# Cache copies by whole rows in packets of 8192 bytes, some of them moved to ScalarE's queue, and later turns in a hybrid decoder step

## Chip, core and metric

The kernel runs on one core of a Trainium2 chip. The metric is the device time of one execution in microseconds (us); lower is better.

## What is computed

One layer of a hybrid decoder, for a prompt group (1 x 512 tokens) and a sample group (8 sequences x 4 tokens, with a past of 2048 rows). In the reference, shortened:

```python
def hybrid_mixer(h, w_in, ..., hist):
    proj = h @ w_in                                   # q, k, v, z, xbc, dt: 1024 -> 5648
    att = [dilated attention(q, k_all, v_all, w, d) for w, d in ((128,1),(512,4),(2048,16))]
    att_out = mix_dilations(att)
    y, h_last = ssd_scan(conv(xbc), dt, A, Bm, Cm, D, h0, chunk)
    out = concat[att_out, gated_rmsnorm(y, z, g)] @ w_out
    keep = max(0, k_all.shape[1] - MAX_WINDOW)
    new_state = (k_all[:, keep:], v_all[:, keep:], ...)   # sample: old cache moved up by 4 rows, 4 new rows
# h <- LN1(ALPHA*h + mixer(h));  h <- LN2(ALPHA*h + PEER(h))
# PEER: queries, top 16 of 128 x 128 product keys, 8 heads, gelu(tok . u[e]) * gate, sum of v[e]
```

For the sample group each new cache (keys and values) is (8, 2048, 1024) in float32: rows 4 to 2047 of the old cache become rows 0 to 2043 of the new one, and four new rows follow. These 2044 rows of 4096 bytes per sequence, for keys and for values, are copied from DRAM to DRAM; nothing in the kernel computes with the copied rows.

## The kernel before, in words

Each engine runs one program of stages, in this order: projections (`sp_project`, `act_project`, `pool_project`, `dve_project`, `pe_project`), attention (`*_attend`), the SSD scan (`*_ssd_run`, `sp_ssd`), the output product with LN1 (`*_out`), the PEER queries with top-k (`*_query`, `dve_topk`), the dense up product beside one-hot gates (`*_up`, `dve_onehots`), and the values product with LN2 (`*_values`, `*_final`). Engines wait for each other on semaphores only.

Weights are float32 split in a high and a low part. SyncE loads a block of 128 x 1024 (512 KB) of w_in into one of four slots, L300; ScalarE rounds it (`hi`, L326), GpSimd subtracts (`lo`, L363), and TensorE multiplies it in three products (`product`, L188 to L190). There are 44 blocks, eleven turns of four slots. ScalarE's cast of block j waits until TensorE has released the slot, so at most four blocks are ahead. The tokens (xraw) are loaded in two halves of four chunks each, L293 and L295, the dt weight between them; ScalarE rounds chunk by chunk (L318, L321), VectorE subtracts (L377, L380).

The cache copies. 2044 rows x 1024 floats per sequence are taken as one run and cut into 16 units (`CHUNK`, L269), a unit into 16 pieces of 32704 bytes. `copy_cache` (L272 to L277) copies one unit of all 8 sequences, with the pieces as outermost dimension, then the sequences: 128 packets of 32704 bytes. `copy_half` (L279 to L283) copies half a unit of the values, 128 packets of 16352 bytes. All add to the semaphore `copied`, and only SyncE's last wait of `sp_values` (L2193) waits for it, for all 48. Where they are issued:

- ScalarE's queue, in `act_project`: after each turn of four weight casts, `copies(x)` (L328) issues a unit of keys and half a unit of values, ten times.
- SyncE's queue: four halves at the end of `sp_attend` (L643); in `sp_ssd` (L981), after the norm gain and the first two states, six units of keys and a half (L987 to L989); in `sp_out`, two halves after each of the first two pairs of w_out loads (L1451, L1452); in `sp_query` a half ahead of each of the twelve later peer_wq loads and one before them (L1623, L1626).

An issue occupies the queue of the engine that makes it; the instructions after it on that engine stand behind it. SyncE does nothing but waits and issues. ScalarE also has the casts, the exponentials of the attention and the copies out of PSUM.

Attention is a loop of 67 rounds (`ROUNDS`): scores of unit n, transposes of unit n-2, values of unit n-3, with the steps of the eight sample sequences between (`sample_steps`). In round `EVERY + 4` of a sequence `dec_turn_out` (L736) turns its output; it waits for VectorE's `d_rows`, and stands ahead of the round's own turn and values.

The SSD scan works on four chunks of 128 tokens and the sample rows. Orders are written out by hand in `pe_ssd`, `act_ssd` and `dve_ssd` (L936 to L950). TensorE's `turn_out` (L1031) transposes the normed rows of chunk i-1 at the end of the loop body of chunk i (L1148). VectorE's `dve_ssd_run` begins with a wait for the norm gain (L1245), which it first uses in `normed` (L1314). In `act_query` (L1700) ScalarE copies each of the 16 queries out of PSUM and rounds a later weight block.

Of the kernel before, what the change touches and what calls it, by code (L numbers as in the profile page):

```python
# [16 lines left out]
D = 1024  # L17
# [131 lines left out]
def layer(nc, t):  # L149

    ctx = ExitStack()
    with ctx:
# [92 lines left out]
        x_in = [sem(f"x_in{s}") for s in range(2)]  # L245
# [23 lines left out]
        CHUNK = (WIN - NT) * D // 16  # L269
        PIECE = CHUNK // 16  # L270

        def copy_cache(eng, side, x):  # L272

            src, dst = (("cache_k", "o_ks"), ("cache_vall", "o_vsall"))[side]
            cutout = lambda ap, lo: ap.rearrange("b s d -> b (s d)")[:, bass.ds(x * CHUNK + lo, CHUNK)]\
                .rearrange("b (s n) -> s b n", n=PIECE)
            eng.dma_start(cutout(t[dst], 0), cutout(t[src], NT * D)).then_inc(copied, 16)  # L277

        def copy_half(eng, y):  # L279

            cutout = lambda ap, lo: ap.rearrange("b s d -> b (s d)")[:, bass.ds(y * (CHUNK // 2) + lo, CHUNK // 2)]\
                .rearrange("b (s n) -> s b n", n=PIECE // 2)
            eng.dma_start(cutout(t["o_vsall"], 0), cutout(t["cache_vall"], NT * D)).then_inc(copied, 16)  # L283

# [5 lines left out]
        def sp_project(sp):  # L292
            sp.dma_start(xraw[:, 0:4], t["xT"][:, 0:4]).then_inc(x_in[0], 16)  # L293
            sp.dma_start(dtw_raw, t["w_dt"]).then_inc(dtw_in, 16)
            sp.dma_start(xraw[:, 4:8], t["xT"][:, 4:8]).then_inc(x_in[1], 16)  # L295
# [19 lines left out]
        def act_project(act):  # L315
            for c in range(DC):
                act.wait_ge(x_in[c // 4], 16)
                act.copy(xs[0][:, c], xraw[:, c]).then_inc(x_hi, 1)  # L318
                if c == 3:
                    act.wait_ge(dtw_in, 16)  # L320
                    act.copy(dtw[0], dtw_raw).then_inc(x_hi, 1)  # L321
# [6 lines left out]
            def copies(x):  # L328
                copy_cache(act, 0, x)
                copy_half(act, x)  # L330
# [17 lines left out]
            with act.Fori(0, 2) as x:  # L348
                for s in range(4):
                    hi(x + 8, s, (rows_ready, x * 10 + (5 if s < 2 else 10)))  # L350
                copies(x + 8)
            for s in range(4):
                hi(10, s, (rows_ready, 20 + (5 if s < 2 else 10)))
# [3 lines left out]
        def pool_project(pool):  # L357
# [9 lines left out]
            pool.wait_ge(x_in[0], 16)  # L367
            pool.wait_ge(x_in[1], 16)
# [5 lines left out]
        def dve_split_x(dve):  # L374
            for c in range(DC):
# [2118 lines left out]
```

## Time and profile before

| what | value |
|---|---|
| median of 3 runs | 2127.38 us (2119.74 to 2133.82) |
| profiled execution, in all | 2123.87 us |
| its span | 2122.0 us |
| PE busy | 2027.4 us (96%) |
| PE weight load busy | 1687.3 us (80%) |
| DVE, ACT, POOL busy | 1488.1, 743.7, 784.4 us |
| bytes moved by DMA | 683.04 MB, mean 322 GB/s |
| HBM read, written | 618.78, 196.32 MB |

PE is TensorE's matmul, DVE VectorE, ACT ScalarE, POOL GpSimd, SP SyncE; SPq and ACTq are the instructions of an engine's queue that issue DMAs, and are not counted as busy. L12 is line 12 of the kernel. A DMA share of 1.00 is all sixteen DMA engines busy. MB and GB are powers of ten; KB of an issue is 1024 bytes. The span runs from the first to the last instruction in the profile.

### The profile page before, as it was taken

The numbers are of one execution on the slowest core, as the hardware profiler recorded it, in microseconds if no ns is written. First come the engines' busy times: TensorE is split into PE (matmuls) and PEld (weight loads), VectorE is DVE, ScalarE is ACT, GpSimd is POOL, SyncE is SP. The second block draws the span as 40 slices with busy tenths as digits, with TensorE's granted clock in tenths as the row PEclk, the third lists the DMA queues.
The fourth block names the chain that finished last, engine by engine and source line by source line (L and its number), as shares of the span: only waits on it lengthen the run. The fifth ranks groups of instructions, "written<-read, shape, count | busy, mean of one in ns | idle before, by whom it ended". The sixth has DMA issues, their size and how long they took to land.

```text
span 2122.0 us, 33482 instructions
## 1 busy us (share of the span) xinstructions
PE 2027.4 (96%) x12142; PEld 1687.3 (80%) x12142; DVE 1488.1 (70%) x3108; ACT 743.7 (35%) x1112; POOL 784.4 (37%) x483
## 2 busy tenths in 40 slices
PE   7999999997989999899999999999989999999998
PEld 7999965554553339899999999999978887777776
DVE  1276135553672335579889699999689898888988
ACT  3232124443440012134343355655333333333332
POOL 4333310000210003248899732122456555555530
PEclk9999999998989999999999999999999999999999
DMA  8999988788998479738999888878999999999993
GB/s 320 343 331 321 314 316 336 307 324 280 321 335 309 163 290 334 288 123 291 353 354 359 285 308 305 305 277 297 395 384 390 392 392 390 390 383 388 382 363 138
DMA packets 202350, 683.04 MB, mean 322 GB/s; under 512 B 18304, under 2 KB 84224, under 8 KB 194176
## 3 DMA queue, kind: packets, MB, share of 16 engines
q1 hardware_dynamic: 150256, 442.42, 58.0%
q0 software_dynamic: 46080, 167.79, 20.7%
q10 hardware_dynamic: 5904, 71.39, 9.8%
q8 instruction: 65, 1.06, 0.2%
q14 instruction: 45, 0.37, 0.0%
HBM read 618.78 MB, written 196.32 MB: 384 GB/s over the span
## 4 chain that ended last, share of the span: by engine, by line
PE 51%; DMA 24%; issue 11%; DVE 7%; POOL 4%; ACT 2%; SPq 0%; POOLq 0%; DVEq 0%; ACTq 0%
DMA overlay<-peer_v 17%; PE bank L188 10%; PE bank L189 9%; PE bank L190 9%; PE bank L1480 5%; PE bank L2082 4%; POOL overlay L363 4%; DVE overlay L2294 2%; PE bank L682 2%; DMA overlay<-peer_wq 2%; PE bank L666 2%; DMA arena<-w_out 1%; DMA overlay<-peer_u 1%; DVE arena L2095 1%; PE bank L732 1%
## 5 line engine op out<-in xcount | busy, mean ns | idle before, releaser
L188 PE MATMUL bank<-overlay 128*128 128x384 f32 (+4 forms) x2768 | 941.5, 340 | 40.3 <-DVE overlay L2300 21.1
L189 PE MATMUL bank<-overlay 128*128 128x384 f32 (+4 forms) x2768 | 926.5, 335 | 0.0
L190 PE MATMUL bank<-overlay 128*128 128x384 f32 (+4 forms) x2768 | 926.2, 335 | 0.0
L188 PEld LDWEIGHTS bank<-overlay 128*128 128x128 f32 (+1 forms) x2768 | 521.3, 188 | 88.5 <-issue 36.4
L190 PEld LDWEIGHTS bank<-overlay 128*128 128x128 f32 (+1 forms) x2768 | 520.6, 188 | 31.5
L189 PEld LDWEIGHTS bank<-overlay 128*128 128x128 f32 (+1 forms) x2768 | 521.4, 188 | 30.3
L1919 POOL DMA_INDIRECT arena<-peer_v,arena x160 | 263.2, 1645 | 223.6 <-DVE arena L2095 206.3
L1640 POOL TENSOR_TENSOR overlay<-overlay 128x1024 fp32r<-128x1024 f32 x86 | 206.6, 2404 | 293.2 <-ACT overlay L1633 289.5
L1633 ACT CAST overlay<-overlay 128x1024 fp32r<-128x1024 f32 x144 | 150.1, 1044 | 160.3 <-DMA overlay<-peer_u 88.2
L2095 DVE SCALAR_TENSOR_TENSOR arena<-arena 128x1024 f32<-128x1024 f32 x160 | 204.9, 1281 | 0.1
L1919 POOL DMA_INDIRECT arena<-peer_rows,arena x80 | 107.3, 1341 | 246.8 <-DVE arena L2090 227.0
L2294 DVE TENSOR_TENSOR overlay<-overlay 128x1024 fp32r<-128x1024 f32 x128 | 156.3, 1221 | 42.8 <-ACT overlay L2202 42.8
L2202 ACT CAST overlay<-overlay 128x1024 fp32r<-128x1024 f32 x128 | 134.4, 1050 | 142.8 <-DMA overlay<-peer_v 140.7
L363 POOL TENSOR_TENSOR overlay<-overlay 128x1024 fp32r<-128x1024 f32 x44 | 106.1, 2422 | 173.0 <-ACT overlay L326 173.0
L1992 ACT ACTIVATE arena<-bank 128x384 f32<-128x384 f32 x128 | 63.9, 499 | 206.5 <-PE bank L190 201.0
L2206 ACT CAST overlay<-overlay 128x384 fp32r<-128x384 f32 x128 | 65.6, 513 | 198.1 <-DVE overlay L2290 198.1
L1480 PE MATMUL bank<-arena 128*128 128x512 f32 x256 | 116.5, 606 | 1.3 <-DMA arena<-w_out 1.3
L2031 ACT COPY arena<-bank 128x512 f32<-128x512 f32 x96 | 104.0, 1135 | 36.0 <-PE bank L2082 36.0
L1780 DVE SCALAR_TENSOR_TENSOR arena<-arena,bank 128x1024 f32<-128x1024 f32 x80 | 96.3, 1213 | 23.0 <-DMA arena<-peer_rows,arena 22.8
L2126 DVE TENSOR_SCALAR arena<-arena 128x128 f32<-128x128 f32 x384 | 106.7, 354 | 0.0
L2082 PE MATMUL bank<-arena 128*128 128x128 f32 x768 | 101.1, 274 | 0.0
L2082 PEld LDWEIGHTS bank<-arena 128*128 128x128 f32 x768 | 99.1, 191 | 0.0
(241 smaller groups left out, 2131.7 us busy)
## 6 DMA issues: line engine op xcount, KB each, us to landing
overlay<-peer_u SPq DMA_DIRECT2D x128, 512.0 KB, 7.2
overlay<-peer_v SPq DMA_DIRECT2D x128, 512.0 KB, 11.5
o_vsall<-cache_vall SPq DMA_DIRECT2D x22, 2044.0 KB, 28.0
o_ks<-cache_k ACTq DMA_DIRECT2D x10, 4088.0 KB, 17.8
arena<-cache_kT SPq DMA_DIRECT2D x32, 896.0 KB, 11.0
arena<-cache_v SPq DMA_DIRECT2D x56, 512.0 KB, 6.5
arena<-w_out SPq DMA_DIRECT2D x48, 512.0 KB, 5.7
act<-arena SPq DMA_DIRECT2D x128, 192.0 KB, 7.8
```

The source lines that it names most:

```text
L188: pe.matmul(out, lhs[0], rhs[0], start=start, stop=False)
L189: pe.matmul(out, lhs[0], rhs[1], start=False, stop=False)
L190: return pe.matmul(out, lhs[1], rhs[0], start=False, stop=stop)
L363: pool.tensor_tensor(ws[1][:, s], wraw[:, s], ws[0][:, s].bitcast(F32), ALU.subtract).then_inc(w_lo, 1)
L1480: mm = pe.matmul(bank[:, 2 * (i % 2) + half, :], mixT[:, c, i * P:(i + 1) * P], w[:, half * 512:(half + 1) * 512], start=(c == 0), stop=(c ...
L1633: act.copy(us[0][:, s], uraw[s]).then_inc(u_hi, 1)
L1640: pool.tensor_tensor(us[1][:, s], uraw[s], us[0][:, s].bitcast(F32), ALU.subtract).then_inc(u_lo, 1)
L1919: pool.indirect_dma_start(gring[g % RING], None, table, bass.IndirectOffsetOnAxis(ap=at, axis=0)).then_inc(row_in[g % RING], 16)
L2082: mm = pe.matmul(bank[:, 4 + w % 4, j * P:(j + 1) * P], hot_b[:, w % 2, j], hot_a[:, w % 2, j], start=True, stop=True)
L2095: dve.scalar_tensor_tensor(acc, gring[r], w[:, bass.ds(j, 1)], acc, ALU.mult, ALU.add).then_inc(row_done, 1)
L2202: act.copy(vs[0][:, j], vraw[:, k]).then_inc(v_hi, 1)
L2294: dve.tensor_tensor(vs[1][:, j], vraw[:, k], vs[0][:, j].bitcast(F32), ALU.subtract).then_inc(v_lo, 1)
```

## The change

- The copies go by whole rows. The 2044 rows are cut into 14 units of 146 rows; a unit is taken as 73 pairs of rows, a pair (8192 bytes) being one packet. The pairs are the outermost dimension of both sides, then the sequences. `copy_cache` copies a unit of keys of all 8 sequences (584 packets), `copy_half` a unit of values of four sequences, the first four or the last four (292 packets). There are 42 copies.
- ScalarE issues nine pairs in `act_project` (not ten); three halves in rounds 47, 51 and 55 of `act_attend`; eleven halves in `act_query`, one after each of the first eleven queries.
- SyncE issues five units of keys and a half in `sp_ssd` and two halves twice in `sp_out`; none in `sp_attend` and `sp_query`.
- The dt weight is loaded, rounded and split first, and the tokens come in four loads.
- `dec_turn_out` goes to the end of its round; the turn of the normed rows of chunk i-1 goes from the end of the body of chunk i to the place after `state` of chunk i+1; VectorE waits for the norm gain only where it uses it first.

```diff
--- before.py
+++ after.py
@@ -242,7 +242,7 @@
         consts_in, dtw_in = sem("consts_in"), sem("dtw_in")
-        x_in = [sem(f"x_in{s}") for s in range(2)]
+        x_in = [sem(f"x_in{s}") for s in range(4)]
         x_hi, x_lo = sem("x_hi"), sem("x_lo")
@@ -266,33 +266,30 @@
         copied = sem("copied")
-        CHUNK = (WIN - NT) * D // 16
-        PIECE = CHUNK // 16
-
-        def copy_cache(eng, side, x):
+        UNITS_OF_CACHE = 14
+        ROWS_OF_UNIT = (WIN - NT) // UNITS_OF_CACHE
+        COPIES = 9 * 2 + 5 + 19
+
+        def copy_rows(eng, side, x, b0, nb):

             src, dst = (("cache_k", "o_ks"), ("cache_vall", "o_vsall"))[side]
-            cutout = lambda ap, lo: ap.rearrange("b s d -> b (s d)")[:, bass.ds(x * CHUNK + lo, CHUNK)]\
-                .rearrange("b (s n) -> s b n", n=PIECE)
-            eng.dma_start(cutout(t[dst], 0), cutout(t[src], NT * D)).then_inc(copied, 16)
-
-        def copy_half(eng, y):
-
-            cutout = lambda ap, lo: ap.rearrange("b s d -> b (s d)")[:, bass.ds(y * (CHUNK // 2) + lo, CHUNK // 2)]\
-                .rearrange("b (s n) -> s b n", n=PIECE // 2)
-            eng.dma_start(cutout(t["o_vsall"], 0), cutout(t["cache_vall"], NT * D)).then_inc(copied, 16)
-
-
-
+            cutout = lambda ap, lo: ap[b0:b0 + nb, bass.ds(x * ROWS_OF_UNIT + lo, ROWS_OF_UNIT)].rearrange("b (s r) d -> s b (r d)", r=2)
+            eng.dma_start(cutout(t[dst], 0), cutout(t[src], NT)).then_inc(copied, 16)
+
+        def copy_cache(eng, x):
+            copy_rows(eng, 0, x, 0, NB)
+
+        def copy_half(eng, x, late):
+            copy_rows(eng, 1, x, late * NB // 2, NB // 2)

...
         def sp_project(sp):
-            sp.dma_start(xraw[:, 0:4], t["xT"][:, 0:4]).then_inc(x_in[0], 16)
             sp.dma_start(dtw_raw, t["w_dt"]).then_inc(dtw_in, 16)
-            sp.dma_start(xraw[:, 4:8], t["xT"][:, 4:8]).then_inc(x_in[1], 16)
+            for k in range(4):
+                sp.dma_start(xraw[:, 2 * k:2 * k + 2], t["xT"][:, 2 * k:2 * k + 2]).then_inc(x_in[k], 16)
             sp.dma_start(oldconv, t["state_conv"]).then_inc(consts_in, 16)
@@ -313,12 +310,11 @@
         def act_project(act):
+            act.wait_ge(dtw_in, 16)
+            act.copy(dtw[0], dtw_raw).then_inc(x_hi, 1)
             for c in range(DC):
-                act.wait_ge(x_in[c // 4], 16)
+                act.wait_ge(x_in[c // 2], 16)
                 act.copy(xs[0][:, c], xraw[:, c]).then_inc(x_hi, 1)
-                if c == 3:
-                    act.wait_ge(dtw_in, 16)
-                    act.copy(dtw[0], dtw_raw).then_inc(x_hi, 1)

@@ -326,8 +322,8 @@
             def copies(x):
-                copy_cache(act, 0, x)
-                copy_half(act, x)
+                copy_cache(act, x)
+                copy_half(act, x, 0)

@@ -345,12 +341,11 @@
                 copies(x + 4)
-            with act.Fori(0, 2) as x:
+            for x in range(8, 11):
                 for s in range(4):
-                    hi(x + 8, s, (rows_ready, x * 10 + (5 if s < 2 else 10)))
-                copies(x + 8)
-            for s in range(4):
-                hi(10, s, (rows_ready, 20 + (5 if s < 2 else 10)))
+                    hi(x, s, (rows_ready, (x - 8) * 10 + (5 if s < 2 else 10)))
+                if x == 8:
+                    copies(x)
             act.wait_ge(sam_used, VG + 1)
@@ -364,20 +359,19 @@
                 lo(0, s)
-            pool.wait_ge(x_in[0], 16)
-            pool.wait_ge(x_in[1], 16)
+            for k in range(4):
+                pool.wait_ge(x_in[k], 16)
             pool.tensor_copy(xsam, xraw[:, :, SEQ:]).then_inc(sam_in, 1)
...
         def dve_split_x(dve):
+            dve.wait_ge(x_hi, 1)
+            dve.tensor_tensor(dtw[1], dtw_raw, dtw[0].bitcast(F32), ALU.subtract).then_inc(x_lo, 1)
             for c in range(DC):
-                dve.wait_ge(x_hi, c + 1 + c // 4)
+                dve.wait_ge(x_hi, c + 2)
                 dve.tensor_tensor(xs[1][:, c], xraw[:, c], xs[0][:, c].bitcast(F32), ALU.subtract).then_inc(x_lo, 1)
-                if c == 3:
-                    dve.wait_ge(x_hi, 5)
-                    dve.tensor_tensor(dtw[1], dtw_raw, dtw[0].bitcast(F32), ALU.subtract).then_inc(x_lo, 1)

@@ -385,7 +379,7 @@
             for c in range(DC):
-                pe.wait_ge(x_lo, 5 if c < 4 else c + 2)
+                pe.wait_ge(x_lo, c + 2)
                 for half in range(2):
@@ -640,8 +634,6 @@
                             values_of(KB * b + kb + 4)
-            for y in range(15, 19):
-                copy_half(sp, y)

@@ -759,8 +751,6 @@
                         dec_scores(b, 2 * at + 1)
-                    if at == EVERY + 4:
-                        dec_turn_out(b)
                 if 2 <= n < UNITS + 2:
@@ -772,6 +762,9 @@
                     values(n - 3)
+                for b, at in sample_steps(n):
+                    if at == EVERY + 4:
+                        dec_turn_out(b)

@@ -889,6 +882,8 @@
             for n in range(ROUNDS):
+                if n in (47, 51, 55):
+                    copy_half(act, (n - 47) // 4, 1)
                 for b, at in sample_steps(n):
@@ -934,8 +929,8 @@
         pe_ssd = Events(sem("pe_ssd"), fronts("x_turned sums") + order((0, "seg0 seg1")) +
-            chunks((0, 0, "state y0 seg2 inter y1 seg3 y2"), (1, 0, "seg0"), (0, 0, "y3"), (1, 0, "seg1"), (0, 1, "out_turned")) +
-            order((QT, "y0 seg2 y1 seg3 y2 y3 out_turned " + by_seq("state") + " last_turned")))
+            chunks((0, 0, "state"), (-1, 1, "out_turned"), (0, 0, "y0 seg2 inter y1 seg3 y2"), (1, 0, "seg0"), (0, 0, "y3"), (1, 0, "seg1")) +
+            order((QT, "y0"), (QT - 1, "out_turned"), (QT, "seg2 y1 seg3 y2 y3 out_turned " + by_seq("state") + " last_turned")))
         act_ssd = Events(sem("act_ssd"), fronts("x_kept b_kept cb_kept eacs etot wexp") + order((0, "E0 E1")) +
@@ -984,9 +979,9 @@
                 sp.dma_start(h0[:, b], t["state_ssm"][b]).then_inc(h0_in[b], 16)
-            for x in range(10, 16):
-                copy_cache(sp, 0, x)
-            copy_half(sp, 10)
+            for x in range(9, UNITS_OF_CACHE):
+                copy_cache(sp, x)
+            copy_half(sp, 9, 0)
             assert stores[0] == 16 * SSD_STORES
@@ -1134,8 +1129,14 @@
             seg(0, 1)
+            def turn_normed(i):
+                dve_ssd.wait(pe, i, "t_inter")
+                pe_ssd.count_done(i, "out_turned", turn_out(pe, i - 1, 0))
+
             for i in range(QT):
                 state(i)
+                if i >= 2:
+                    turn_normed(i - 1)
                 intra(i, 0)
@@ -1145,10 +1146,8 @@
                 seg(i + 1, 1)
-                if i:
-                    dve_ssd.wait(pe, i, "t_inter")
-                    pe_ssd.count_done(i, "out_turned", turn_out(pe, i - 1, 0))
             intra(QT, 0)
+            turn_normed(QT - 1)
             seg(QT, 2)
@@ -1242,7 +1241,6 @@
         def dve_ssd_run(dve):
-            dve.wait_ge(normg_in, 16)
             dve.wait_ge(consts_in, 96)
@@ -1316,6 +1314,8 @@
                 dve_ssd.wait(dve, i, "rstd")
+                if i == 0:
+                    dve.wait_ge(normg_in, 16)
                 if i:
@@ -1448,8 +1448,8 @@
                 if i < 2:
-                    copy_half(sp, 2 * i + 11)
-                    copy_half(sp, 2 * i + 12)
+                    copy_half(sp, 2 * i + 10, 0)
+                    copy_half(sp, 2 * i + 11, 0)
             pe_ssd.wait(sp, QT - 1, "inter")
@@ -1620,10 +1620,8 @@
                 sp.dma_start(uraw[s], t["peer_wq"][s]).then_inc(u_in[s], 16)
-            copy_half(sp, 19)
             with sp.Fori(1, QF // 4) as k:
                 for s in range(4):
-                    copy_half(sp, k * 4 + (16 + s))
                     sp.wait_ge(u_lo, k * 4 + (s - 3))
@@ -1699,13 +1697,17 @@
             act.sem_inc(q_kept, 2)
-            with act.Fori(0, QF // 4) as k:
-                for s in range(4):
-                    f = k * 4 + s
-                    act.wait_ge(q_ready, f + 1)
-                    act.wait_ge(s_ready, f + 1)
-                    act.copy(qT[:, s % 2].rearrange("p (h n) -> p h n", h=2), bank[:, 2 * (s % 2):2 * (s % 2) + 2, 0:HALF]).then_inc(q_kept, 1)
-                    hi_of(act, s, k + 1)
+            def query(k, s):
+                f = k * 4 + s
+                act.wait_ge(q_ready, f + 1)
+                act.wait_ge(s_ready, f + 1)
+                act.copy(qT[:, s % 2].rearrange("p (h n) -> p h n", h=2), bank[:, 2 * (s % 2):2 * (s % 2) + 2, 0:HALF]).then_inc(q_kept, 1)
+                hi_of(act, s, k + 1)
+
+            for f in range(QF):
+                query(f // 4, f % 4)
+                if f < 11:
+                    copy_half(act, 3 + f, 1)
             for g in range(1, FOLD):
@@ -2190,7 +2192,7 @@
             group(PAIRS - 1, 1)
-            sp.wait_ge(copied, 16 * 48)
+            sp.wait_ge(copied, 16 * COPIES)

```

## Rows read from the trace of the kernel before

**Rows 1.** The page, part 3: all packets, then packets, MB and share by queue.
```profile
DMA packets 202350, 683.04 MB, mean 322 GB/s; under 512 B 18304, under 2 KB 84224, under 8 KB 194176
...
q1 hardware_dynamic: 150256, 442.42, 58.0%
q0 software_dynamic: 46080, 167.79, 20.7%
q10 hardware_dynamic: 5904, 71.39, 9.8%
```

**Rows 2.** Windows by stage: length, busy us (count) by engine, PEclk, DMA share, GB/s.
```profile
12.00:290.00 278.00, 274.70 (x2250) 264.40 (x2248) 109.43 (x182) 67.08 (x72) 106.47 (x45) 1.00 0.93 324
...
517.00:606.00 89.00, 75.94 (x327) 46.69 (x326) 53.11 (x62) 36.73 (x68) 21.39 (x20) 0.92 0.98 327
...
787.00:905.00 118.00, 106.23 (x782) 98.91 (x782) 65.48 (x316) 26.12 (x35) 37.91 (x16) 0.96 0.86 312
905.00:2122.00 1217.00, 1183.67 (x6331) 1080.93 (x6330) 1063.62 (x2120) 494.06 (x639) 615.34 (x390) 0.99 0.91 333
```

**Rows 3.** DMA issues: transfer, queue, count, KB each, median us to landing.
```profile
arena<-peer_rows,arena POOLq DMA_INDIRECT x160, 7.4
arena<-peer_v,arena POOLq DMA_INDIRECT x160, 9.1
...
o_ks<-arena SPq DMA_DIRECT2D x8, 16.0 KB
o_vsall<-arena SPq DMA_DIRECT2D x8, 16.0 KB
```

**Rows 4.** Timeline of SyncE's queue, 500 to 650 us: start, us taken, line.
```profile
517.90 0.34 SPq L984 DMA_DIRECT2D arena<-ssm_norm_g  x1
...
610.38 6.52 SPq L283 DMA_DIRECT2D o_vsall<-cache_vall  x2
616.94 8.83 SPq L1437 DMA_DIRECT2D arena<-w_out  x3
625.88 5.70 SPq L1458 DMA_DIRECT2D arena<-ln_g  x1
```

**Rows 5.** DMA view of 527 to 560 us: packets, mean rate, share of 16 engines.
```profile
DMA packets 524, 11.06 MB, mean 335 GB/s; under 512 B 57, under 2 KB 57, under 8 KB 203
...
q1 hardware_dynamic: 523, 11.05, 100.0%
```

**Rows 6.** DMA view of 275 to 285 us.
```profile
DMA packets 876, 4.13 MB, mean 413 GB/s; under 512 B 186, under 2 KB 186, under 8 KB 766
...
q1 hardware_dynamic: 873, 4.11, 99.3%
```

**Rows 7.** Timeline of ScalarE, 222 to 256 us.
```profile
224.37 0.60 ACTq L277 DMA_DIRECT2D o_ks<-cache_k  x1
```

**Rows 8.** The chain of waits over the whole span: start us, us, what.
```profile
609.01 31.26 DMA arena<-w_out
640.32 3.70 PE bank L1480 x8
648.07 3.63 PE bank L1480 x8
...
827.11 35.86 DMA overlay<-peer_wq
```

**Rows 9.** Timeline of TensorE, 0 to 20 us.
```profile
11.42 0.41 PE L188 MATMUL bank<-overlay 128*16 128x272 f32 x1 [11.42 <-DVE overlay L380]
```

**Rows 10.** TensorE's waits, 500 to 650 us: us in all, times, longest.
```profile
PE bank L1064 <- DVE arena L1254: 8.6, 1, 8.6
PE bank L1035 <- DVE arena L1323: 7.7, 3, 3.3
```

## Prediction

> **What bounds the kernel now.** I read the page first. TensorE is busy in nearly every slice, and beside it the sixteen DMA engines are busy for 58.0 + 20.7 + 9.8 = 88.5% of the span [rows 1]. So two resources are close to full, and which one ends a stage differs. The busy times by stage [rows 2] show it: in the projections (12 to 290 us) PE is busy 274.70 of 278 us with DMA at 0.93; in the SSD scan (517 to 606) PE has holes (75.94 of 89) with DMA at 0.98; in the query stage (787 to 905) PE is busy 106.23 of 118; from 905 on, 1183.67 of 1217. The reader is to see that TensorE sets the pace wherever its operands come in time, and that they do so because each transfer is moved by sixteen engines at once. The cache copies are 2 x 8 x 2044 rows of 4096 bytes, 134 MB of the 683.04 MB. Nothing computes with them; they are filler in the DMA engines' time, and the kernel waits for them only at its last instruction. They cost nothing as long as (a) they are spread evenly and (b) the queue that issues them is never full.
>
> **How a copy is dealt over the engines.** This is the step on which all else hangs. On POOL's queue 320 gathers of 128 rows left 46080 packets [rows 1, 3]: 144 each, the 128 rows and 16 more, one for each engine. I count all issues of the DMA view: 745 on SP's queue, 43 on ACT's, 320 on POOL's, 1108. Sixteen small packets each make 17728; six of the constants and of o_conv have 128 rows under 512 B, 768 more; together 18496. The page has 18304 [rows 1], 192 fewer, and 192 is 16 x 12. The sixteen stores of 16 KB [rows 3] are the only DMAs whose outermost dimension has 4 rows (all others have 128, 32 or 16). So a transfer with 4 outermost pieces ran on 4 engines and left 4 small packets, not 16: the outermost dimension is what is dealt out. Before the change a copy has 16 outermost pieces, one an engine. After it, `"b (s r) d -> s b (r d)"` with r=2 cuts 146 rows to s = 73, and 73 is outermost on both sides. The rows allow three rules for 73: as even a deal as 128, 32, 16 and 4 all got (73 is prime, so an even deal exists on one engine only); an uneven deal over 15 or 16; or over a few. I take the even one, since every transfer in the trace is one. Then a key unit is 73 x 8 = 584 packets of 8192 bytes on one engine, a value half 292, and all copies 14 x 584 + 28 x 292 = 16352 packets on that engine.
> The Trainium skill, page "DMA: Bandwidth & Descriptors", section "Why a DMA increments its semaphore by 16 and not by 1", states just this: the engines used are the largest number up to 16 that divides the slowest dimension of both sides, with 127 partitions giving 1. The trace agrees as far as it reaches (4 rows, 4 engines); no transfer here has a count that 16 and 4 don't divide.
>
> **What a full queue does.** An issue of a DMA takes SP 0.34 us when the queue is short (the norm gain at 517.90 us) [rows 4]. In the timeline of SP's queue at 610 us [rows 4] two copy halves take 6.52 us to issue, three w_out loads 8.83 us, one norm load 5.70 us, while the 27 MB of copies issued at 519 to 526 us have, at 335 GB/s [rows 5], just ended (81 us). Outstanding then were one store, six loads or so and four halves, 8 data packets an engine each: some 70 an engine. From there on each issue waits until as many packets are gone as it adds. So the issuing queue takes some 70 packets an engine ahead, and a copy of 584 packets on one engine holds SyncE or ScalarE until all but some 70 are moved. ScalarE's casts and activations stand behind it.
>
> **Price of a packet.** From 527 to 560 us only copies run: 335 GB/s with all 16 busy [rows 5], 20.9 GB/s an engine, 0.392 us for 8192 bytes. From 275 to 285 us, mostly loads, 413 GB/s at 99.3% [rows 6]: 25.8 GB/s an engine, 0.3175 us. With one engine at work the memory is nearly idle, so I take 0.3175 us and keep 0.392 as the other end. All copies: 16352 x 0.3175 = 5192 us, or 6410 us.
>
> **The sum, stage by stage** (profiled execution: span 2122.0 us, 2123.87 us in all, 3.5 us under the median of the runs).
> - Projections. ScalarE issues nine pairs (keys and half the values), 9 x 876 = 7884 packets, 2503 us. Before, ten pairs went out here between the casts, at 0.6 us an issue; the last but one stands at 224.37 us [rows 7]. While ScalarE is held, PE has the four weight blocks already split, 25 us of work; when it is freed the next four casts go in about 10 us, before the 70 packets (22 us) left are moved, so the engine never rests. The weight blocks pass the same engine: 36 x 8 packets of 4096 bytes, 46 us. From 17 us: 17 + 2503 + 46 - 22 = 2544 us when ScalarE is free; then what was left at 224 us of the 290, less the 25 us: 41 us. The stage ends at 2585 us in place of 290: +2295.
> - Attention. Three halves on ScalarE at rounds 47, 51, 55: 3 x 292 x 0.3175 = 278 us, less 22 us tail, less 8 rounds at 227/67 us done meanwhile (26): +230. Behind the blocked issue stand the exponentials and the copies of the turned tiles, so PE stops.
> - SSD scan and output. SyncE issues five key units and a half (3212 packets, 1020 us) where six units and a half went, then twice two halves (1168 packets, 371 us) among the w_out loads, all on one queue in order. The SSD's 89 us lie beside this. w_out 4 lands at 519 + 1020 + 371 + 5 = 1915 us of the old scale; PE wanted it at 640 + 4 x 7.7 = 671 us (w_out is used every 648.07 - 640.32 = 7.7 us) [rows 2, 8]: +1244.
> - Query. ScalarE issues eleven halves, one after each query: 11 x 292 x 0.3175 = 1020 us, with the peer_wq packets on that engine 14 us more, less the tail 22 us, then five queries at 118/16 = 7.4 us, and 8 us before the first: 1057 us in place of 118: +939. The 35.86 us chain on peer_wq [rows 8] no longer has copies ahead of it in SP's queue, but PE's idle time there is 118 - 106.23 = 11.8 us at most [rows 2] and lies inside this stretch.
> - From 905 us on nothing is changed: +0.
> Sum 2295 + 230 + 1244 + 939 = 4708; 2123.87 + 4708 = 6832. I forecast 6830 us. At 0.392 us a packet it is 16352 x 0.0745 = 1218 more, 8050 us.
>
> **The other edits.** The dt weight first and the tokens in four parts: PE's first matmul starts at 11.42 us [rows 9]; gain 0 to 3 us, and under ScalarE's first block nothing. DVE's wait for the norm gain moved back: PE waited 8.6 us for it at 517 to 529 us [rows 10]; out of order turns (the out_turned move): 7.7 us in 3 waits [rows 10]; dec_turn_out later: 0 to 2 us. Together 0 to 21 us if the copies stay spread. In my forecast they lie beside SyncE's 1020 us and are worth 0. If a turn is now late it adds less than a us each, hidden likewise. Smaller packets (8192 for 32704 bytes) let weight packets through sooner where two queues share an engine.
>
> **Rivals.**
> 1. Spread after all, faster: 73 is dealt unevenly over 15 or 16 engines. Place: SSD start, output turns, query. Then no issue blocks (37 to 40 packets an engine for a key unit, under 70), the 8.6 us, half of the 7.7 (3.9) and two thirds of the 11.8 (7.9) come back: 2124 - 20 = 2104 us. It decides if an uneven deal exists at all. For it: nothing in the rows forbids it. Against: every counted transfer was dealt evenly.
> 2. Spread and no gain: the same, but the DMA engines at 0.98 in the SSD scan [rows 2] just shift the wait to w_out: 2120 us.
> 3. One engine, but its queue takes everything and no issuer is held. Then the loads, a sixteenth of which pass the same engine, alternate with copies; what is left is the engine's own work: 5192 us of copies and (683 - 134)/16 = 34.3 MB at 25.8 GB/s, 1330 us: 6520 to 6700 us. Against: the 6.52 us issues [rows 4].
>
> **How the numbers follow.** Forecast 0.78, rival 1 0.09, rival 2 0.05, rival 3 0.08. A measurement of this kernel tells about 1% from no change. Faster 0.09, same 0.05, slower 0.86. The likeliest case runs from 6450 us (a deeper queue, packets a little under 0.3175 us) to 8100 us (0.392 us); rival 3 lies inside, and the two spread cases, 0.14, are left out.
>
> **What would show it.** Right: a DMA busy share near one engine in sixteen (0.06) and 25 GB/s over thousands of us; issues of o_ks<-cache_k of 160 to 185 us each; ScalarE's first casts after 250 us gaps; chain of waits through the copies' issues or w_in, w_out and peer_wq; packets under 512 B down by 48 x 16 - 42 = 726, less 32 for two more token loads. Wrong: o_ks issues near 1 us and mean GB/s near 320 (rivals 1, 2); short issues with long landings (rival 3). A packet time off 0.3175 us scales 5192 us of the sum.

## The result and the profile after

| | before | after |
|---|---|---|
| median | 2123.56 us (4 runs, 2117.81 to 2133.82) | 6636.41 us (4 runs, 6635.41 to 6637.03) |
| ratio | 1 | 3.1306, 95% interval 3.1198 to 3.1413 |

The forecast was 6830 us, with a range from 6450 to 8100 us. The page of the changed kernel, parts 1 to 3 (what they answer to: [rows 1]):
```profile
span 6634.9 us, 33385 instructions
...
PE 2108.5 (32%) x12142; PEld 1737.3 (26%) x12142; DVE 1484.6 (22%) x3108; ACT 741.7 (11%) x1112; POOL 779.6 (12%) x483
...
DMA  1000000000000037110000001250000019889998
GB/s 68 39 39 27 39 27 39 39 27 39 27 39 39 27 129 278 60 45 27 27 27 27 27 36 45 72 179 33 33 30 33 33 69 344 310 295 376 389 390 293
DMA packets 212120, 683.04 MB, mean 103 GB/s; under 512 B 17610, under 2 KB 83530, under 8 KB 193994
...
q1 hardware_dynamic: 150902, 407.14, 16.8%
q0 software_dynamic: 46080, 167.79, 6.6%
q10 hardware_dynamic: 15028, 106.67, 3.9%
```
The same 683.04 MB are moved and the engines do the same work; VectorE, ScalarE and GpSimd are busy as long as before. But slice after slice shows 27 GB/s, near the rate of one of the sixteen DMA engines (in the projections before, 413 GB/s over sixteen are 25.8 each [rows 6]). TensorE (PE) is busy 81.1 us longer for the same 12142 matmuls; the last section comes back to that. 17610 packets under 512 B are 694 fewer than the 18304 of before. 48 copies with 16 small packets each became 42 with one each (726 fewer), and two more token loads add 32: 18304 - 726 + 32 = 17610, to the last packet.

The timeline of ScalarE's queue (start us, us taken, line; before, such an issue took 0.60 us [rows 7]):
```profile
16.90 1.32 ACTq L277 DMA_DIRECT2D o_ks<-cache_k  x1
18.25 159.99 ACTq L277 DMA_DIRECT2D o_vsall<-cache_vall  x1
...
194.73 78.75 ACTq L277 DMA_DIRECT2D o_ks<-cache_k  x1
273.63 178.19 ACTq L277 DMA_DIRECT2D o_vsall<-cache_vall  x1
452.28 1.04 ACT L322 CAST overlay<-overlay 128x1024 fp32r<-128x1024 f32 x1 [256.74 <-issue]
```
178.19 us is 584 packets at 0.3051 us, 26.8 GB/s. It is the issue of a half, which itself has 292 packets. So what an issue waits for is that the packets of the DMAs before it, here a key unit of 584, have gone. The first key unit was taken whole in 1.32 us. The half after it waited 159.99 us, which at 0.3051 us is 524 packets, so it was let in with some 60 left (an estimate). The next cast of ScalarE stands 256.74 us behind "issue", which is the profile's word for time in which an engine waited for nothing that it shows.

SyncE's queue in the SSD stage and among the w_out loads (against [rows 4]):
```profile
2871.36 764.67 SPq L277 DMA_DIRECT2D o_ks<-cache_k  x5
3636.08 178.29 SPq L277 DMA_DIRECT2D o_vsall<-cache_vall  x1
3814.42 87.71 SPq L262 DMA_DIRECT2D o_hp<-arena  x1
3902.18 7.28 SPq L1437 DMA_DIRECT2D arena<-w_out  x2
```
TensorE's waits over the whole span (us in all, times, longest):
```profile
PE bank L1480 <- DMA arena<-w_out: 1302.8, 3, 962.6
PE bank L188 <- POOL overlay L358: 1223.6, 7, 250.2
PE bank L1687 <- ACT arena L1704: 789.5, 10, 95.7
PE bank L428 <- POOL overlay L358: 737.5, 3, 249.9
PE bank L402 <- ACT arena L332: 150.0, 1, 150.0
PE bank L674 <- ACT arena L861: 131.9, 2, 77.6
```
L358 is GpSimd's split, L1704, L332 and L861 are ScalarE's copies out of PSUM; none of them is slow. Each stands behind ScalarE's held issue, directly or over one more engine. The first row is SyncE's case: a load that left late, in the same queue as the copies.

### The profile page after: what moved, and what is told of

It is laid out like the page before. It is cut to its first block, busy times and chain, and to the rows that moved or that the text cites. A ratio compares the mean times of both kernels' runs of the same rounds, so it can differ in the third digit from the quotient of the medians.

```text
span 6634.9 us, 33385 instructions
## 1 busy us (share of the span) xinstructions
PE 2108.5 (32%) x12142; PEld 1737.3 (26%) x12142; DVE 1484.6 (22%) x3108; ACT 741.7 (11%) x1112; POOL 779.6 (12%) x483
## 2 busy tenths in 40 slices
DMA packets 212120, 683.04 MB, mean 103 GB/s; under 512 B 17610, under 2 KB 83530, under 8 KB 193994
## 4 chain that ended last, share of the span: by engine, by line
issue 51%; SPq 16%; PE 16%; DMA 9%; another core or an unknown queue 5%; DVE 2%; POOL 1%; ACT 1%; ACTq 0%; POOLq 0%; DVEq 0%
SPq L277 14%; DMA overlay<-peer_v 6%; PE bank L188 3%; PE bank L189 3%; PE bank L190 3%; PE bank L1480 2%; SPq L262 1%; PE bank L2084 1%; DMA arena<-prompt_bias 1%; POOL overlay L358 1%; DVE overlay L2296 1%; PE bank L674 1%; PE bank L658 1%; PE bank L724 0%
## 5 line engine op out<-in xcount | busy, mean ns | idle before, releaser
L188 PE MATMUL bank<-overlay 128*128 128x384 f32 (+4 forms) x2768 | 957.6, 346 | 1325.6 <-POOL overlay L358 1223.6
L189 PE MATMUL bank<-overlay 128*128 128x384 f32 (+4 forms) x2768 | 940.2, 340 | 0.0
L190 PE MATMUL bank<-overlay 128*128 128x384 f32 (+4 forms) x2768 | 938.7, 339 | 0.0
L188 PEld LDWEIGHTS bank<-overlay 128*128 128x128 f32 (+1 forms) x2768 | 535.4, 193 | 1378.0 <-issue 1264.7
L189 PEld LDWEIGHTS bank<-overlay 128*128 128x128 f32 (+1 forms) x2768 | 535.3, 193 | 30.2
L190 PEld LDWEIGHTS bank<-overlay 128*128 128x128 f32 (+1 forms) x2768 | 533.7, 193 | 31.3
L1480 PEld LDWEIGHTS bank<-arena 128*128 128x128 f32 x256 | 49.5, 200 | 1369.1 <-issue 1026.3
L358 POOL TENSOR_TENSOR overlay<-overlay 128x1024 fp32r<-128x1024 f32 x44 | 104.1, 2384 | 2296.6 <-ACT overlay L322 2296.6
L1687 PE MATMUL bank<-arena 128*128 128x128 f32 x128 | 27.2, 380 | 789.5 <-ACT arena L1704 789.5
L1687 PEld LDWEIGHTS bank<-arena 128*128 128x128 f32 x128 | 23.7, 277 | 792.6 <-ACT arena L1704 792.4
L322 ACT CAST overlay<-overlay 128x1024 fp32r<-128x1024 f32 x44 | 44.4, 1040 | 1090.3 <-issue 1048.4
L1631 ACT CAST overlay<-overlay 128x1024 fp32r<-128x1024 f32 x144 | 150.1, 1044 | 92.2 <-DMA overlay<-peer_u 88.7
```

What stands on the lines that cost most here:

```text
L188: pe.matmul(out, lhs[0], rhs[0], start=start, stop=False)
L189: pe.matmul(out, lhs[0], rhs[1], start=False, stop=False)
L190: return pe.matmul(out, lhs[1], rhs[0], start=False, stop=stop)
L358: pool.tensor_tensor(ws[1][:, s], wraw[:, s], ws[0][:, s].bitcast(F32), ALU.subtract).then_inc(w_lo, 1)
L1480: mm = pe.matmul(bank[:, 2 * (i % 2) + half, :], mixT[:, c, i * P:(i + 1) * P], w[:, half * 512:(half + 1) * 512], start=(c == 0), stop=(c ...
L1631: act.copy(us[0][:, s], uraw[s]).then_inc(u_hi, 1)
```

## Where the time went, by stage

A stage is taken from the start of one instruction that both kernels have to the next: the first cache_kT load (294.6 us before, 2422.9 after), the load of the norm gain (517.9, 2870.0), the first peer_wq load (779.7, 4423.2), ScalarE's last query copy (924.7, 5369.5), the end (2122.0, 6634.9).

| stage | before | after | more | forecast |
|---|---|---|---|---|
| projections | 294.6 | 2422.9 | 2128.3 | 2295 |
| attention | 223.3 | 447.1 | 223.8 | 230 |
| SSD, output | 261.8 | 1553.2 | 1291.4 | 1244 |
| queries | 145.0 | 946.3 | 801.3 | 939 |
| rest | 1197.3 | 1265.4 | 68.1 | 0 |

Together 4512.9 us, the difference of the spans. The last row was not forecast. The timeline of ScalarE after its last query copy shows what it is:
```profile
5369.49 48.81 ACTq L1712 DMA_DIRECT2D arena<-arena  x1
5418.34 17.40 ACTq L1712 DMA_DIRECT2D arena<-arena  x2
```
The three small folding DMAs stand behind the last copy half in ScalarE's queue, 66 us. ScalarE's program of the up product comes after them, and with it the first increment of `gelu_done` (L1988), for which TensorE waits 63.8 us once.

## The experiments

**Theory and rivals.** Theory: the outermost dimension of a transfer is dealt evenly, over the largest number of engines up to 16 that divides it; 73 is prime, so one engine, and the issuers are held. Rivals: the new places on ScalarE's queue cost the time; packets of 8192 bytes or the 8 MiB steps between sequences are slow; a count that 16 doesn't divide falls to one engine or is dealt by its common factor with 16.

**1. e1_even64**, 64 equal pieces in place of 73 pairs of rows; units, queues and places stay.
```diff
-            cutout = lambda ap, lo: ap[b0:b0 + nb, bass.ds(x * ROWS_OF_UNIT + lo, ROWS_OF_UNIT)].rearrange("b (s r) d -> s b (r d)", r=2)
-            eng.dma_start(cutout(t[dst], 0), cutout(t[src], NT)).then_inc(copied, 16)
+            unit = ROWS_OF_UNIT * D
+            cutout = lambda ap, lo: ap[b0:b0 + nb].rearrange("b s d -> b (s d)")[:, bass.ds(x * unit + lo, unit)]\
+                .rearrange("b (s n) -> s b n", s=64)
+            eng.dma_start(cutout(t[dst], 0), cutout(t[src], NT * D)).then_inc(copied, 16)
```


> The changed kernel with one thing altered: a unit is cut into 64 equal pieces of 9344 bytes, in place of 73 pairs of rows of 8192 bytes; units, queues and places stay. Theory (an even deal over the largest number up to 16 that divides the outermost count): 64 goes to 16 engines, 32 packets an engine for a key unit, no issue takes more than a few us, small packets up by 42 x 15 = 630, and the time comes back to 2085 to 2125 us (I take 2104). Rival (the small packets, the 8 MiB steps between sequences, or ScalarE's queue hold the copies up, whatever the outermost count): stays over 4000 us.

Measured: 2122.48 us, ratio to before 1.0005 (0.9981 to 1.0029). The new cut took back all of the 4513 us. With the count it also changes the packets, from 8192 to 9344 bytes, and they no longer follow whole rows; runs 3 and 5 set these apart. Its DMA view:
```profile
DMA packets 210735, 683.04 MB, mean 322 GB/s; under 512 B 18241, under 2 KB 84161, under 8 KB 194625
```
There are 631 more small packets than 17610, where 630 were forecast. The "few us" for an issue did not hold: five key units on SyncE's queue took 38.39 us and the half behind them 16.15 us to issue. The five now put 160 packets on each engine where six had put 48. SyncE has nothing else to do then. Nor did the 20 us of gain show; runs 7 and 8 below go after that.

**2. e2_even16**, s=16 in the same place: 16 pieces of 37376 bytes.

> The changed kernel with a unit cut into 16 pieces of 37376 bytes. Theory: 16 engines, time near the 64 piece version's, at most 1% over it, since larger packets let the loads of SyncE through less often. Rival (large packets hold up the loads seriously): over 2150 us. Rival (the deal is not what counts): over 4000 us.

Measured: 2141.85 us, 1.0071 (1.0050 to 1.0091). As the theory has it, with a cost of 0.9% over the 64 pieces. w_in landed 20.6 us after its issue in the median, with 64 pieces 12.7 us, before 17.6 us. In these three the load on the other queue gets through sooner the smaller the copies' packets are (37376, 9344 and 32704 bytes). That is no rule for any size: with the 8176 byte pieces of run 9 it took 27.7 us.

**3. e3_before73**, the kernel before with one number changed.
```diff
-        PIECE = CHUNK // 16
+        PIECE = CHUNK // 73
```


> The kernel before with one number altered: a unit is cut into 73 pieces of 7168 bytes (halves: 3584), in place of 16 of 32704; queues and places as before. Theory: everything on one engine; 134 MB at 26.85 GB/s (584 packets of 8192 bytes in 178.2 us) are 4989 us, of which some 450 us lie beside other work: 6500 to 6900 us, with small packets down by 48 x 15 = 720 to 17584. Rival (the new places on ScalarE's queue are what costs): under 3000 us.

Measured: 6716.27 us in one execution, and
```profile
DMA packets 223518, 683.04 MB, mean 102 GB/s; under 512 B 17584, under 2 KB 83504, under 8 KB 221488
```
17584 small packets, as forecast. Neither the new places nor the new share of ScalarE in the copies is needed for the loss: the count does it in the old places too.

**4. e4_rows146**, `r=2` becomes `r=1`: single rows, 146 outermost.

> The changed kernel with single rows as packets of 4096 bytes, so that 146 = 2 x 73 is outermost. Theory: two engines, half the bytes on each, 2490 us of copies at 26.85 GB/s (2600 at 0.159 us a packet), some 400 to 480 us of it hidden: 4130 to 4350 us, small packets 17610 + 42 = 17652. Rival (an outermost count that 16 does not divide falls to one engine): about 6600 us or, with packets of 4096 bytes, more. Rival (uneven deal once there are many pieces): about 2110 us.

Measured: 4192.79 us in one execution. The page has two engines' rate in slice after slice, and the small packets again to the last one:
```profile
GB/s 113 71 70 70 53 70 70 70 53 71 71 72 244 321 134 79 53 53 53 53 66 79 192 186 66 61 62 61 119 347 356 299 287 302 390 391 390 390 385 248
DMA packets 228514, 683.04 MB, mean 163 GB/s; under 512 B 17652, under 2 KB 83572, under 8 KB 226740
```
An issue of a half behind a key unit took 90.40 us: 584 packets of 4096 bytes on each of two engines at 0.155 us. Smaller packets on twice the engines cost 2444 us less.

**5. e5_pairs72**, to tell "largest divisor" from "common factor with 16" and from the size of the count.
```diff
-        ROWS_OF_UNIT = (WIN - NT) // UNITS_OF_CACHE
-        COPIES = 9 * 2 + 5 + 19
+        ROWS_OF_UNIT = 144
+        COPIES = 9 * 2 + 5 + 19 + 2
...
+            copy_rest(sp)
```
(`copy_rest` issues the last 28 rows of keys and of values, 14 pairs outermost.)

> The changed kernel with units of 144 rows, 72 pairs outermost, and the 28 rows left of keys and of values in two more copies of 14 pairs at the end of sp_ssd. Theory (largest divisor up to 16): 72 goes to 12 engines and 14 to 14; small packets 17610 - 42 + 42 x 12 + 2 x 14 = 18100, and since each of the 12 engines has 11.2 MB of copies for 8.4 MB before, 2110 to 2180 us. Rival (largest common factor with 16): 8 engines and 2, small packets 17908, over 2180 us. Rival (nearly even deal over 15 or 16): small packets 18226 or more. If 73 is bad for its size and not for its divisors, 72 must be bad too: over 6000 us.

Measured: 2135.44 us in one execution, before at 2117.67 us. Its DMA view:
```profile
DMA packets 212610, 683.04 MB, mean 320 GB/s; under 512 B 18100, under 2 KB 84020, under 8 KB 194484
```
18100: twelve engines for 72 pieces, fourteen for 14. With the 4, 16, 32 and 128 of before, and 73, 146 and 64, nine counts fall under the one rule, and neither rival rule fits them all. The packets are the 8192 byte pairs of whole rows of the changed kernel, so their size and form are not what costs. This kernel is what the change set out to be, within 1% of before.
The Trainium skill, "DMA: Bandwidth & Descriptors", section "Why a DMA increments its semaphore by 16 and not by 1", states the rule in these terms, the largest divisor up to 16. These runs agree with it at 73 (1), 146 (2), 14 (14), 72 (12) and 64 (16).

**6. e9_nocopies**: the 48 copies and the wait for them are left out of the kernel before.

> The kernel before without any cache copy (48 DMAs and the last wait left out; rows 0 to 2043 of the two new caches are not written). It prices the copies when they are spread: if they are only filler, at least 2100 us; if they hold up loads where DMA is at 0.9 and more, 2040 to 2090 us. With it the hidden part of the 4989 us is known: the changed kernel's 6636 less this, less 4989.

Measured: 2096.86 us, 0.9906 (0.9876 to 0.9936): between the two ranges, a little under the 2100 us of "only filler". Spread over sixteen engines, 134 MB cost 21 us (the prediction has them cost nothing); on one engine they cost 6636 - 2097 = 4539 us. At 0.3051 us for each of 16352 packets the copies last 4989 us, so 450 us of them were hidden. The windows of this run (length, busy, PEclk, DMA share, GB/s) show the room the copies fill:
```profile
12.00:290.00 278.00, 276.56 (x2252) 265.15 (x2250) 113.51 (x182) 66.49 (x73) 106.40 (x45) 1.00 0.28 99
...
517.00:606.00 89.00, 82.40 (x366) 49.51 (x365) 60.52 (x69) 41.57 (x76) 23.81 (x24) 1.00 0.16 56
```
In the projections TensorE is busy 276.56 us with DMA at 0.28, against 274.70 us at 0.93 with the copies [rows 2].

**7. e8_edits_alone**: all edits but those on the copies.
```diff
+            for k in range(4):
+                sp.dma_start(xraw[:, 2 * k:2 * k + 2], t["xT"][:, 2 * k:2 * k + 2]).then_inc(x_in[k], 16)
...
+                if i >= 2:
+                    turn_normed(i - 1)
...
-            dve.wait_ge(normg_in, 16)
```


> The kernel before with the small edits alone (dt weight first, tokens in four loads, later dec_turn_out, moved turn of the normed rows, later wait for the norm gain); all copies as before. The prediction priced them at 0 to 21 us. I take 2103 to 2124 us, 10 us gained, with the 8.6 us wait at 517 to 529 us gone. Rival: the holes are filled by waits for w_out, which comes no sooner: within 4 us of before.

Measured: 2119.69 us, 1.0013 (0.9986 to 1.0041): no gain that could be measured. The time lies in the ranges of both, and the trace decides. TensorE's waits from 500 to 650 us, against [rows 10]:
```profile
PE bank L1484 <- DMA arena<-w_out: 17.8, 2, 12.0
PE bank L1105 <- DVE arena L1275: 4.0, 2, 3.5
...
PE bank L1034 <- DVE arena L1327: 0.7, 2, 0.4
PE bank L1063 <- DVE arena L1256: 0.7, 1, 0.7
```
The edits do what they say: the wait of 8.6 us behind the norm gain is 0.7, the three of 7.7 us are 0.7. In their place TensorE reaches w_out sooner and waits 17.8 us for it, 1.3 us before. The first pair of w_out loads is issued 14 us sooner (592.38 us, before 606.34), but TensorE can use it only 4.4 us sooner (625.0 for 629.4), and the next pair no sooner at all (641.73 for 640.32). The copies have to do with it: without any (run 6) TensorE doesn't wait for w_out here, and the wait behind the norm gain is 1.8 us and not 8.6. The rival of this run holds, and with it the step of the prediction's second rival, that the wait shifts to w_out.

**8. e10_halves_on_sp and e13_halves_beside_out**: the 64 piece version with copies moved. In the first, the three halves of rounds 47, 51 and 55 go to the end of `sp_attend`. In the second they and the four halves of `sp_out` go into ScalarE's `act_out`:
```diff
+                if n < 4:
+                    copy_half(act, 10 + n, 0)
+                if n < 3:
+                    copy_half(act, n, 1)
```


> The 64 piece version with the three value halves of the attention rounds issued by SyncE at the end of sp_attend in place of ScalarE in rounds 47, 51 and 55. In the 64 piece version the attention stage was some 11 us longer than before. Theory (the copies beside cache_kT and cache_v hold those up): the 11 us come back there but the SSD stage gets 7.2 MB more, w_out is later by up to 10 us: 2110 to 2125 us. Rival (the moved dec_turn_out is what lengthened the stage): 2122 us, no change.

> The 64 piece version with seven halves (three of the attention rounds, four of sp_out) issued by ScalarE one or two at a time during the output product, where DMA was busy at 0.67 to 0.70. They no longer stand ahead of w_out in SyncE's queue. Theory (what the small edits win in the SSD stage is given back to waits for w_out, 16.3 us in 3 waits): 2095 to 2112 us, w_out waits under 8 us. Rival (the copies only move the wait to the output product or the queries): 2118 to 2135 us.

Measured: 2118.64 us, 0.9985 (0.9965 to 1.0006), and 2134.64 us, 1.0063 (1.0040 to 1.0087). The first is no different from before that could be measured, and its time can't tell theory from rival. The traces can. From the first cache_kT load to the norm gain the attention takes 235.0 us in the 64 piece version (290.49 to 525.49) and 225.3 us in this one (290.55 to 515.89), so 10 us come back; and run 7, which has the moved `dec_turn_out` and not the new copies, takes 219.8 us, before 223.3. So the rival is out. As the theory has it, the w_out waits grew in return, from 16.3 to 22.6 us.

The second failed; its waits:
```profile
PE bank L1477 <- DMA arena<-w_out: 20.8, 6, 9.2
PE bank L188 <- DVE overlay L2303: 19.1, 20, 5.5
PE bank L188 <- POOL overlay L1639: 17.4, 2, 16.1
```
The w_out waits became more, not fewer: 20.8 us in 6, where the 64 piece version has 16.3 us in 3, and the first query block is 16.1 us late as well. So it isn't enough that no half stands ahead of w_out in its own queue. That copies on the other queue hold these loads up as well is likely, and was not shown by itself. The rival held: the wait moves. No version with all the copies is faster than the kernel before by more than its interval; without any copy there are only 21 us to be had.

**9. e6_before64, e11_before112, e12_off16**: the size of the pieces. The first two change one number of the kernel before (`CHUNK // 64`, `CHUNK // 112`), the third shortens each piece of the 64 piece version (`bass.ds(x * unit + lo, unit - 256)`).

> The kernel before with a unit in 64 pieces of 8176 bytes (halves: 4088) in place of 16 of 32704: smaller packets alone, queues and places as they were. If packets of ScalarE's queue alternate with those of SyncE's loads, w_in lands sooner than 17.6 us after its issue (I take 8 to 14), and the time falls by 0 to 12 us: 2112 to 2124. Rival: more packets an engine (32 for a key unit) fill the queue, SyncE is held in the SSD stage, and the time rises by 5 to 20 us.

> The kernel before with a unit in 112 pieces of 4672 bytes (halves: 2336), in place of 16. The version with 64 pieces of 8176 bytes took 2714 us, and the DMA engines were busy at 0.95 while moving 218 GB/s. Theory A (pieces that end off a 64 byte line are slow when many engines write side by side: 8176 = 16 x 511): 4672 = 64 x 73 and 2336 = 32 x 73 are cut better, so 2110 to 2250 us though the pieces are smaller. Theory B (small packets with 8 MiB steps, or neighbours 32704 bytes apart, are slow): 7 x 4672 is again 32704 bytes an engine, the pieces are smaller, so 2700 us or more.

> The changed kernel with 64 pieces a unit, each 16 bytes shorter: 9328 bytes = 16 x 583, in place of 9344 = 128 x 73 (the last 1024 bytes of each unit and sequence are not copied). Theory A (alignment): rises from 2122 us to 2500 to 3000 us, mean GB/s in the first 700 us near 220. Theory B (distance, size, steps): those are all but unchanged, so 2110 to 2135 us.

Measured: 2713.73 us, 1.2715 (1.2641 to 1.2789); 2251.13 us; 2175.67 us (the last two in one execution each). All three missed, the second by 1 us: it lies just above the range of its theory A, and far from theory B. The windows from 12 to 290 us, where the projections stand, in this order: 64 pieces of 9344 bytes (e1_even64), then e6_before64, e11_before112 and e12_off16.
```profile
12.00:290.00 278.00, 276.56 (x2262) 265.99 (x2261) 107.13 (x180) 67.86 (x71) 106.31 (x45) 1.00 0.94 331
```
```profile
12.00:290.00 278.00, 171.68 (x1233) 167.16 (x1232) 66.25 (x107) 43.49 (x49) 62.54 (x27) 0.80 1.01 166
```
```profile
12.00:290.00 278.00, 249.30 (x1974) 239.61 (x1973) 104.26 (x169) 62.79 (x69) 96.00 (x41) 0.96 0.96 273
```
```profile
12.00:290.00 278.00, 249.07 (x1992) 241.62 (x1991) 100.43 (x169) 63.33 (x67) 99.42 (x42) 0.94 1.00 289
```
The DMA engines are near full in all four (0.94 to 1.01), and move 331, 166, 273 and 289 GB/s. With pieces of 8176 (16 x 511) and 4088 (8 x 511) bytes they do half of what they do with 9344 (128 x 73). It is not the number of packets: 112 smaller pieces, 4672 (64 x 73) and 2336 (32 x 73) bytes, do better. It is not the deal either: the two kernels have 18304 small packets like the kernel before, sixteen for each copy. Pieces of 9328 (16 x 583) bytes, cut no finer than 8176, lose 13% and not half, so 16 bytes less in length and step cost something, but far from all of it. Whether that is a matter of alignment was not shown, and what else slows the 8176 byte pieces is open; their distance was not tried by itself.

## Why the prediction was right

- **How a copy is dealt.** Right, and shown: the count of the small packets to the last one in the changed kernel and in runs 3, 4 and 5, and the time taken back by run 1 alone.
- **A full queue holds its issuer.** Right in kind, wrong in form. I had an issue wait until its own packets but 70 were gone. It waits until those of the DMAs before it are, but for some 60, and is then taken whole: 178.19 us for a half of 292 packets behind a unit of 584. So the sign "issues of o_ks<-cache_k of 160 to 185 us" did not come: behind a half they took 78.75 us and the like, and it was the halves that took 178. The last half of a series leaves 292 + 60 = 352 packets, 107 us, beside other work, not 70, 22 us. By this reckoning 85 us more were hidden in the projections and 85 in the queries. The 70 was a slip too: the eleven DMAs of 8 packets listed for it make 88, and the seven that were out before the 6.52 us issue [rows 4] make 56, near the measured 60.
- **Price of a packet.** Mis-sized: 0.3175 us taken, 0.3051 measured. 16352 x 0.0124 = 203 us. That this is nearly the 194 us between forecast and result is luck: three tails of 85 us, in the projections, the attention and the queries, took off 255 us more, and what the next three points name put some 260 us back. The pure copies of 527 to 560 us [rows 5], nearest in kind, were the worse guide. The argument that one engine alone is quicker than one of sixteen fits 0.3051 us beside 0.392 us; what slows the sixteen was not shown.
- **The stages.** Projections: 98 us less by the packet and 85 by the tail make 183, and 167 were missing. Queries: 40 and 85 make 125, 138 were missing. The attention fits its forecast (223.8 for 230) by luck. The three halves held ScalarE for 155 us only:
```profile
2645.79 0.67 ACTq L277 DMA_DIRECT2D o_vsall<-cache_vall  x1
2657.46 73.11 ACTq L277 DMA_DIRECT2D o_vsall<-cache_vall  x1
2741.67 81.10 ACTq L277 DMA_DIRECT2D o_vsall<-cache_vall  x1
```
  TensorE waited 131.9 us for it. The rest I had not in the sum. TensorE waits 31.7 us for cache_kT and 18.6 us for cache_v (before 1.7 and 1.5), and 18.2 us for VectorE's L788 (4.0); and it is busy 244.92 us (2420 to 2871 us, granted clock 0.70) where it was 210.52 (290 to 517, 0.96).
- **SSD and output:** 54 us less by the packet, yet 47 us more were measured. Of these 101, some 60 are the attention's last half, let in at 2822.8 us with 107 us of packets left, 60 of them beside SyncE's copies on that engine. The rest was not taken apart.
- **The folding DMAs,** 66 us, were a step I left out: after each copy I asked who stands behind it on ScalarE, but not for the last one.
- **The other edits** worth nothing here: right. In the first rival I gave them 20 us if the copies are spread. Run 1 gave 0: the waits at the SSD start did go, and w_out took them. Had the copies been spread, the first rival would have been mis-sized, and the second (spread, no gain: 2120 us) is what the 64 piece version did, 2122 us.
- **Rival 3** (the queue takes everything) fell by the timeline, though its 6520 to 6700 us hold the result: one engine's own work bounds the time either way, so the time alone could not have told them apart.

## What to carry to other kernels

Before a transfer's access pattern is changed, look at its outermost count on both sides: in every run here, on SyncE's and ScalarE's queues, the largest divisor up to 16 is the number of engines that it ran on, and "whole rows" of a length like 2044 = 4 x 7 x 73 easily leave one. A count of the smallest packets on the page checks it. A transfer that nothing waits for can still cost, once its queue is long: name what stands behind its issue on that engine, after the last one too. And where DMA and TensorE are both near full, a wait that is removed can be paid again at the next load, here w_out.

## What the runs showed of the hardware that was not expected

- A DMA is taken whole by a short queue, 584 packets on one engine in 1.32 us, and the next one waits until some 60 are left (159.99 us, 524 packets at 0.3051 us).
- One engine copying DRAM to DRAM alone moves 26.8 GB/s with packets of 8192 bytes; with all sixteen copying it was 20.9 each [rows 5].
- In the windows of the changed kernel the granted TensorE clock is 0.56 over the first 2420 us, near the lower of its two levels (1.2 of 2.4 GHz), with PE busy 299.13 of them. From 12 to 290 us before, with PE busy 274.70 of 278, it is 1.00 [rows 2]. PE's busy time rose from 2027.4 to 2108.5 us for the same 12142 matmuls:
```profile
0.00:2420.00 2420.00, 299.13 (x2257) 284.15 (x2258) 110.79 (x187) 70.57 (x80) 104.90 (x51) 0.56 0.10 39
```
- Pieces of 8176 and 4088 bytes on sixteen engines halve the rate at a full DMA share (166 GB/s at 1.01), where 9344 bytes give 331 GB/s at 0.94. The cause is open.
